# Dealing the token columns of a hybrid decoder step anew: where meta tokens and samples sit

## The reference, cut to what matters

```
h   = rmsnorm(x)                                    # all tokens
p   = h @ w_in                                      # q_a f_a i_a g_a | conv q,k,v | a b | z | gate_a gate_b
o_a = gated linear recurrence (HGRN2) of q_a, f_a, i_a      # prompt in chunks, samples one step
o_b = gated delta rule of conv(q,k,v), a, b                 # prompt in chunks, samples one step
mix = (sigmoid(gate_a) * (norm(o_a) silu(g_a)) @ w_oa + sigmoid(gate_b) * (norm(o_b) silu(z)) @ w_ob) @ w_out
x   = x + mix
x   = x + moe(rmsnorm(x))                           # top 4 of 32 experts, SwiGLU
y   = rmsnorm(x)                                    # y_prompt = tokens 16.. of the prompt, y_sample
```

## Time and profile before

| | us |
|---|---|
| three timed executions | 1292.35, 1294.76, 1291.99; median 1292.35 |
| profiled execution, from the first to the last instruction (span) | 1290.7 |
| TensorE busy | 1229.7 (95%) |
| VectorE busy | 511.5 (40%) |
| ScalarE busy | 241.9 (19%) |
| GpSimd busy | 69.2 (5%) |
| bytes moved | 450.59 MB, 349 GB/s over the span |

### The profile page before, as it was taken

The page is one execution under the profiler, slowest core; times in us unless marked ns, Lnnn a source line. Parts: engine busy times, 40 slices in busy tenths (PEclk is TensorE's granted clock), DMA queues, the critical chain, the costliest instruction groups (busy, mean ns, idle before and its releaser), DMA issues.

```text
span 1290.7 us, 19040 instructions
## 1 busy us (share of the span) xinstructions
PE 1229.7 (95%) x7387; PEld 554.9 (43%) x7387; DVE 511.5 (40%) x1055; ACT 241.9 (19%) x411; POOL 69.2 (5%) x149
## 2 busy tenths in 40 slices
PE   7999989989999999999999999999999999999996
PEld 5887756655433333333333333333333333333331
DVE  1183776254554333333333333333333333333345
ACT  3223611321611111111111111111111111111103
POOL 3002002001210000000000000000000000000001
PEclk9999999999999999999999999999999999999999
DMA  9343307419799999999999999999999999999991
GB/s 305 132 141 129 133 7 208 173 52 365 303 397 408 429 429 427 429 430 429 427 429 430 429 427 429 430 429 427 429 429 429 427 429 429 429 427 430 428 429 70
DMA packets 60854, 450.59 MB, mean 349 GB/s; under 512 B 9234, under 2 KB 18568, under 8 KB 35880
## 3 DMA queue, kind: packets, MB, share of 16 engines
q1 hardware_dynamic: 55748, 446.17, 83.7%
q10 hardware_dynamic: 5068, 3.89, 1.2%
HBM read 443.88 MB, written 6.26 MB: 349 GB/s over the span
## 4 chain that ended last, share of the span: by engine, by line
DMA 41%; PE 25%; DVE 2%; issue 2%; SPq 0%; ACT 0%; DVEq 0%; ACTq 0%
DMA ring<-in_w_gu 41%; PE ps L1070 17%; PE ps L1100 4%; PE ps L1033 1%; PE ps L1010 1%; DVE x_tok L1859 1%; PE ps L1049 1%; DVE proj L1834 0%; DVE proj L1828 0%; PE ps L1057 0%; DVE x_tok L1925 0%; PE ps L1024 0%; SPq L390 0%; DVE feat L1833 0%; PE ps L1041 0%
## 5 line engine op out<-in xcount | busy, mean ns | idle before, releaser
L1070 PE MATMUL ps<-ring,feat 128*64 128x512 f32 x1568 | 355.5, 595 | 22.2 <-DMA ring<-in_w_gu 21.9
L1100 PE MATMUL ps<-ring,proj 128*64 128x512 f32 x992 | 237.7, 601 | 0.0
L1070 PEld LDWEIGHTS ps<-ring,feat 128*64 128x64 f32 x1568 | 107.9, 136 | 205.8 <-issue 169.5
L1859 DVE TENSOR_TENSOR x_tok<-x_tok,ps 96x512 f32<-96x512 f32 x192 | 122.7, 679 | 79.9 <-PE ps L1033 77.1
L1827 DVE TENSOR_SCALAR proj<-ps 128x512 f32<-128x512 f32 x32 | 22.1, 691 | 304.8 <-PE ps L1070 303.8
L1100 PEld LDWEIGHTS ps<-ring,proj 128*64 128x64 f32 x992 | 62.1, 136 | 109.6 <-issue 101.8
L1368 ACT ACTIVATE proj<-ps,wide 128x512 f32<-128x512 f32 x32 | 22.0, 687 | 433.1 <-DVE wide L1842 423.1
L661 PE MATMUL ps<-feat,ring 128*128 128x280 f32 x384 | 97.0, 404 | 0.0
L629 PE MATMUL ps<-feat,ring 128*128 128x280 f32 x384 | 93.5, 406 | 0.2 <-DVEq L1434 0.2
L629 PEld LDWEIGHTS ps<-feat,ring 128*128 128x128 f32 x384 | 74.1, 194 | 19.1 <-DVE feat L1433 0.5
L661 PEld LDWEIGHTS ps<-feat,ring 128*128 128x128 f32 x384 | 71.2, 191 | 19.6 <-issue 3.3
(11 more groups left out here) (383 smaller groups left out, 1084.2 us busy)
## 6 DMA issues: line engine op xcount, KB each, us to landing
ring<-in_w_gu SPq DMA_DIRECT2D x96, 2048.0 KB, 25.0
ring<-in_w_down SPq DMA_DIRECT2D x62, 2048.0 KB, 23.4
proj<-in_w_gu SPq DMA_DIRECT2D x15, 2048.0 KB, 25.9
states<-in_w_gu SPq DMA_DIRECT2D x15, 2048.0 KB, 24.9
ring<-in_w_in SPq DMA_DIRECT2D x11, 2048.0 KB, 8.8
ring<-in_w_gu SPq DMA_DIRECT2D x4, 1024.0 KB, 7.7
ring<-in_w_in SPq DMA_DIRECT2D x2, 1024.0 KB, 8.6
out<-states SPq DMA_DIRECT2D x1, 2048.0 KB, 8.7
```

Source lines behind the costliest of these rows:

```text
L1070: last = mm(bank(j // 2)[64 * (j % 2):64 * (j % 2) + 64, :], xgT[:, k % 4, k // 4, :], w[:, 512 * j:512 * j + 512], start=False, stop=k == ...
L1100: last = mm(bank(y)[64 * j:64 * j + 64, :], h[:, k % 4, 64 * (k // 4):64 * (k // 4) + 64], w[:, n:n + 512], start=False, stop=k == KT - 1)
L1859: tt(x, x, bank(banks[i][j])[0:TP, :], ALU.add).then_inc(sg["comb_taken"], 1)
```

## The change

Columns are dealt anew: 8 empty ones, the 16 meta tokens (from `S0` = 8), the 8 samples (from `SA` = 24), the 256 of the prompt (from `SE` = 32). Still 288 columns and nine chunks. What only makes queries or gates (the chunks in `QUERY`, the output tiles, the merge) works on the 264 columns from `SA`. Mix, router, experts and stores see three tiles of 128, 128 and 8 rows (`ROWS`), taken in the order samples, tile 0, tile 1 (`TILES`). The samples' decays are zeroed in the chunk that they share with the meta tokens, the convolution's history is copied over them, and chunk 0 gives no outputs but the samples'. Blocks beyond one per expert are at most 16 in place of 18. Besides, Sync loads expert 0's third pair and down ahead of the wait for the output tiles, the order of the mix is rewritten, the bias transfers are issued ahead of step B's copies on ScalarE, the store of the sample states ahead of chunk 8, `less(0)` stands between merges, GpSimd's constants are made as soon as step B is done, and the router's selection of tile pairs is done tile by tile.

```diff
-    LEAD = 16
-    S0 = LEAD - NS
-    T = LEAD + NM + SEQ
+    S0 = 8
+    SA = S0 + NM
+    SE = SA + NS
+    T = SE + SEQ
...
+    TQ = T - SA
...
+    X_ROWS = (128, 128, SE)
+    X_COL = (SE, SE + 128, 0)
+    QUERY = (0, 3, 7, 8, 9, 10, 11)
+    ROWS = (128, 128, NS)
+    TILES = (2, 0, 1)
+    TOK = (0, 128, 256)
...
+        def first_col(n):
+            return SA if ORDER[n // 4] in QUERY else S0
...
-            sp.wait_ge(sg["oab_done"], KT)
...
-            for q in range(2):
-                gu_load2(0, q)
-
             sp.wait_ge(sg["gB_done"], NCH)
-            sp.wait_ge(sg["prompt_stored"], 32)
             gu_load2(0, 3)
             sp.wait_ge(sg["conv_stored"], 144)
             for q in range(2):
                 down_load(0, q)
-            sp.wait_ge(sg["merged_ready"], KT)
+            sp.wait_ge(sg["oab_done"], KT)
+            for q in range(2):
+                gu_load2(0, q)
+            sp.wait_ge(sg["wout_lo_used"], 1)
+            gu_load2(0, 2)
+            sp.wait_ge(sg["mix_done"], 5)
+            spare_load(1, 0)
+            sp.wait_ge(sg["lg_done"], NI)
             spare_load(1, 1)
-            sp.wait_ge(sg["mix_done"], 2 * NI)
-            gu_load2(0, 2)
...
-                sp.dma_start(y_prompt[0, 2 * TP - 32:2 * TP + 64, 512 * j:512 * j + 512], x_tok[:, NI - 1, 512 * j:512 * j + 512]) \
-                    .then_inc(sg["out_stored"], 16)
-            sp.wait_ge(sg["out_stored"], 16 * (NI + 2))
+            sp.wait_ge(sg["f_ready"], 2)
+            sp.dma_start(y_prompt[0, 0:128, :], x_tok[:, 0, :]).then_inc(sg["out_stored"], 16)
+            sp.wait_ge(sg["f_ready"], 3)
+            sp.dma_start(y_prompt[0, 128:256, 0:512], x_tok[:, 1, 0:512]).then_inc(sg["out_stored"], 16)
+            sp.wait_ge(sg["f_rest"], 1)
+            sp.dma_start(y_prompt[0, 128:256, 512:D], x_tok[:, 1, 512:D]).then_inc(sg["out_stored"], 16)
+            sp.wait_ge(sg["f_ready"], 4)
+            sp.wait_ge(sg["f_rest"], 2)
+            sp.dma_start(y_sample[:, 0, :], x_tok[0:NS, 2, :]).then_inc(sg["out_stored"], 16)
+            sp.wait_ge(sg["out_stored"], 64)
...
+            for g0, g1, n in ((Q_, F_, SA), (F_, G_, S0), (G_, QB_, SA), (QB_, Z_, S0), (Z_, NFT, SA)):
+                L(gp.memset(proj[:, g0:g1, 0:n], 0.0))
...
-            pool.wait_ge(sg["prompt_stored"], 32)
-            pool.wait_ge(sg["oab_done"], KT)
-            pool.wait_ge(sg["merged_ready"], KT)
+            pool.wait_ge(sg["vnew_done"], NCH)
+            pool.wait_ge(sg["oB_done"], NCH)
+            pool.wait_ge(sg["gB_done"], NCH)
             iot = lambda out, pattern, base, mult: L(gp.iota(out, pattern=pattern, base=base, channel_multiplier=mult,
                                                              allow_small_or_imprecise_dtypes=True))
+            L(gp.memset(lower, -1.0))
+            for q in range(2):
+                masked(lower[:, q:q + 1], [[0, 1]], -NE * (q + 1), 1)
+            gp.sem_inc(sg["route_consts"], 1)
...
+                    last = mm(bank(4 + n % 4)[:, 0:T - c0], win_buf[n // 4 % NRING][:, k, 128 * (n % 4):128 * (n % 4) + 128],
+                              feat[:, k, c0:T], start=k == 0, stop=k == KT - 1)
                 last.then_inc(sg["ptile_done"], 1)
...
-            for n in range(NCH):
+            for n in range(1, NCH):
...
-                    last = mm(bank(b)[:, 0:TN], w[:, k, 128 * m:128 * m + 128], proj[:, g + k, S0:T], start=k == 0, stop=k == H - 1)
+                    last = mm(bank(b)[:, 0:TQ], w[:, k, 128 * m:128 * m + 128], proj[:, g + k, SA:T], start=k == 0, stop=k == H - 1)
...
-                    attend(0, v_new0)
-                    sample_read(4, False).then_inc(sg["oB_done"], 1)
+                    sample_read(4).then_inc(sg["oB_done"], 1)
...
-            def mix(b, t0, t1, j, k0, k1):
+            def w_mix(k, d0, n):
+                return (wout_lo[:, k, :] if k < 4 else wout_hi[:, k - 4, :])[:, d0:d0 + n]
...
+            def mix(i, j, k0, k1):
                 for k in range(k0, k1):
-                    last = mm(bank(b)[0:t1 - t0, :], feat[:, k, t0:t1], w_mix(k, j), start=k == 0, stop=k == KT - 1)
+                    last = mm(bank(4 * i + j), feat[:, k, SE + 128 * i:SE + 128 * i + 128], w_mix(k, 512 * j, 512),
+                              start=k == 0, stop=k == KT - 1)
...
+            def mix_samples(k0, k1):
+                for k in range(k0, k1):
+                    for g in range(4):
+                        last = mm(bank(3)[C * g:C * g + NS, 0:256], feat[:, k, SA:SE], w_mix(k, 256 * g, 256),
+                                  start=k == 0, stop=k == KT - 1)
...
             for j in range(2):
-                mix(j, 0, 128, j, 0, 4)
-            pe.wait_ge(sg["wout2_in"], 16)
+                mix(0, j, 0, 4)
             pe.wait_ge(sg["merged_ready"], KT)
             for j in range(2):
-                mix(j, 0, 128, j, 4, KT)
-            mix_pair(2, 128)
+                mix(1, j, 0, 4)
+            mix_samples(0, 4).then_inc(sg["wout_lo_used"], 1)
+            pe.wait_ge(sg["wout2_in"], 16)
+            mix_samples(4, KT).then_inc(sg["mix_done"], 1)
+            mix(0, 0, 4, KT)
+            turn_samples()
+            mix(0, 1, 4, KT)
+            logits(0)
+            mix(1, 0, 4, KT)
             for j in range(2):
                 turn_x2(0, j)
-            mix(4, 2 * TP, T, 0, 0, KT)
-            for j in range(2):
-                turn_x2(1, j)
-            logits(0)
-            mix(5, 2 * TP, T, 1, 0, 4)
+            mix(1, 1, 4, 6)
+            turn_x2(1, 0)
             logits(1)
-            turn_x2(2, 0)
...
+            mix(1, 1, 6, KT)
+            pe.wait_ge(sg["route_consts"], 2)
+            count_ranks(0)
+            count_ranks(1)
+            turn_x2(1, 1)
...
             L.tell(f(wideh(1), ps[:, 0:H, 0:T], ACT.Copy, scale=-1.0), "wT_taken")
+            for p in range(3):
+                act.dma_start(b_f32[NE * p:NE * p + NE, 0:2 * D], b_gu[0]).then_inc(sg["bias_in"], 16)
+                act.dma_start(b_f32[NE * p:NE * p + NE, 2 * D:3 * D], b_down[0]).then_inc(sg["bias_in"], 16)
...
-            act.dma_start(gdn_sample[0].rearrange("b h k v -> k (b h) v"), states[:]).then_inc(sg["stB_stored"], 16)
+                    act.dma_start(gdn_sample[0].rearrange("b h k v -> k (b h) v"), states[:]).then_inc(sg["stB_stored"], 16)
...
-            for p in range(3):
-                act.dma_start(b_f32[NE * p:NE * p + NE, 0:2 * D], b_gu[0]).then_inc(sg["bias_in"], 16)
-                act.dma_start(b_f32[NE * p:NE * p + NE, 2 * D:3 * D], b_down[0]).then_inc(sg["bias_in"], 16)
...
-            act.wait_ge(sg["prompt_stored"], 32)
...
             def less(i):
                 dve.wait_ge(sg["b3_ready"], i + 1)
                 L.tell(stt(out=b_f32, in0=b3, scalar=lower[:, i:i + 1], in1=b_f32, op0=ALU.mult, op1=ALU.add),
                        "b3_less", i + 1)
 
+            for m in range(KT):
+                t0 = proj[:, VB_ + m % 2, SA:T]
+                dve.wait_ge(sg["oab_done"], m + 1)
+                L(tt(t0, bank(m)[:, 0:TQ], proj[:, GB_ + m, SA:T], ALU.mult))
+                L.tell(tt(feat[:, m, SA:T], t0, proj[:, GA_ + m, SA:T], ALU.add), "merged_ready", m + 1)
+                if m == 4:
+                    dve.wait_ge(sg["route_consts"], 1)
+                    less(0)
+            less(1)
...
+            dve.wait_ge(sg["route_consts"], 2)
+            add_samples()
+            root(0)
             add_mix(0, 0)
+            dve.wait_ge(sg["route_in"], 32)
             add_mix(0, 1)
-            less(1)
+            select(0)
+            root(1)
...
             add_mix(1, 0)
+            take_xT(1)
+            select(1)
             add_mix(1, 1)
...
-            take_xT(0)
-            dve.wait_ge(sg["route_in"], 32)
-            root(0)
-            root(1)
-            add_mix(2, 0)
-            take_xT(1)
-            select(0)
-            select(1)
-            L(ts(selb[:, 0:2], selm[:, 0:2], FAR, -FAR, ALU.mult, ALU.add))
```

546 lines of the change are left out of this document (281 added, 265 removed).

## The result

| | before | after |
|---|---|---|
| median of the timed executions, us | 1292.49 (4 runs) | 1300.99 (4 runs: 1299.54 to 1302.28) |
| span of the profiled execution | 1290.7 | 1298.1 |
| start of the output tiles / of the mix | 289.06 / 304.23 | 286.12 / 300.44 |
| gate_up(0) starts | 353.42 | 353.75 |
| first slot given back | 355.40 | 357.43 |

The changed kernel is slower: ratio 1.0057, 95% interval 1.0045 to 1.007. I had forecast 1283.2 with a range up to 1289.2; the measured time lies outside it and on the other side, where I had put 0.05.

The account below looks back on a forecast made before the run. The expert-weight stream, started by gate_up(0), was taken to fix the end; 4.35 us up to the output tiles, 4.0 in the mix and 0.8 at the end sum to 9.15, giving 1283.2 us, range 1279.5 to 1289.2.

Parts of the forecast that it names:

- (e): Step B: six bias transfers moved on ScalarE's queue delay v_new; 3.1 us lost, bounds 2.6 and 5.3.
- (f): Mix: fewer matmul passes and a new order bring gate_up(0) 4.0 us earlier, bounds 0.5 and 4.4.
- (g): Expert loop: same bytes and passes, 128 rows cost VectorE no more than 96; zero change.
- slower rival: Expert loop: TensorE becomes the bound, in combine and add_back of `down`; needs 1.2 us more an expert; chance 0.05.
- the marks at the end: Mix: mix(1,1) ends at 339.5, last logits at 342.9, select(2) at 344.65, gate_up(0) 4.8 us behind select's last TENSOR_REDUCE.
- (a) to (d): Ahead of the mix, gains: narrower columns 5.1 us, output tiles 1.5, first chunk 0.45, start 0.4.
- my terms for that part: Column gains: 2.6 us up to 164.5 us, 0.4 in step A before 178, 1.3 to 226.5.
- The stream follows gate_up(0): Weight stream: the last prefill lands about 4.4 us sooner and the first slot returns 4.0 sooner, so gate_up(0) sets it.
- (h): Program end: one 32 KB store behind the last norm in place of two; 0.8 us gained, bounds 0.3 and 1.2.

Follow-up runs that it names:

- pad128: Changed kernel with the samples' tile given 128 contraction rows, zeros behind the eighth, in the expert loop's pick_rows and turn_share; 1292.4 us, 0.9987 to 1.0008 of before.
- fill_wait: Changed kernel plus four unused matmuls of 128 rows by 512 columns in TensorE's wait in the mix; 1299.15 us.
- warm: all3 plus unused dense matmuls: five of 256 columns in chunk 7 of step B, three of 512 near the last transposes and logits(2); 1286.46 us.
- best3: best1 plus two unused matmuls of 512 columns, behind the ranks of tile 0 and in the middle of logits(2); 1282.53 us.
- all3: Changed kernel with the loop's samples' tile padded to 128 rows, bias transfers issued by Sync, and take_xT(2) copied before the places; 1284.51 us.
- xt_first: Changed kernel with VectorE's copy take_xT(2) put ahead of place(0) and place(1); 1298.41 us, 1.0027 to 1.0049 of before.
- bias_early: Kernel before with the six bias transfers issued on ScalarE right behind wT_taken; 1298.65 us, 1.0031 to 1.0062 of before.
- best2: best1 with the changed kernel's VectorE order and the 12 row-picking matmuls for the first expert between the halves of logits(2); 1285.46 us.
- nocols: all3 without the narrower projection tiles, all 48 at 280 columns again; 1288.51 us, 0.9954 to 0.9986 of before.
- best1: all3 with the samples' tile also at 128 contraction rows in the rows picked ahead of the loop; 1279.18 us, again 1280.44.

## Why the prediction was wrong, point by point

By spans: forecast 9.15 us gained, measured 7.4 lost, a miss of 16.6. About half of it came ahead of the loop (gate_up(0) at 353.75, forecast 345.1: steps (e) and (f)) and half in the loop (8.0 by pad128: step (g)).

- **(g) Expert loop, the largest step that failed.** "Same bytes, same passes of 512 columns; 128 rows in place of 96 cost VectorE nothing ... Zero." I counted passes and looked at VectorE, and not at what a third tile of 8 rows, put between two of 128, does to TensorE's matmuls: 0.96 us an expert. pad128 gives 8.0 us of span for it. I had found TensorE to be 23.5 us ahead of the stream at 1199.36; 26 steps of 0.96 (25.0) and an end of the first of them 5.5 later (447.36, before 441.90) are 30.5, so that mark comes 7.0 later, at 1206.35. My slower rival had the right bound (TensorE) and the wrong place (`down`) and price (1.2 us an expert as threshold). That threshold took the full 8.35 us of earlier start for granted; without it 0.96 was enough. (Its 1301 for 1.5 us more is also too low by its own terms: 29 x 1.5 less 23 and 8.35 is 12.2 us, 1304.5.)
- **(f) The mix.** Forecast 4.0 sooner, measured 4.1 longer (53.3 against 49.2). The terms that I had worked out stood: first halves 13.8, samples 3.6 (314.26 to 317.90; forecast 3.5). The Trainium skill's 2.38 for three column tiles (page "TensorE: Matmul & The Clock Gate", section "Measured speedup vs the span model") would have made it 4.4, an estimate; the row decides for full overlap of four. What failed are the marks at the end, and that I took the clock's 1.00 for granted. Counted from the first mix matmul, the last mix piece ended at 36.0 us (forecast 35.3), the last logits at 42.1 (38.7), and gate_up(0) started at 53.3 (45.2). In fill_wait, warm and best3 dense matmuls in that stretch kept the clock at 1.00 for longer. That thin work alone brings it down is not shown, since the kernel before held it through the end of its mix. Why VectorE's copy came late: `place(0)`'s first operation took 1.70 us while GpSimd worked, and ended with GpSimd's operation (339.01 and 338.97); in all3 and xt_first it took 0.18. That the two hinder each other there was seen, not tested.
- **(e) Bias transfers.** The step was right in kind and sized too low: forecast 3.1 lost, 2.77 of issues measured, but 6.35 in all (bias_early) and 5.8 in the changed kernel (from 219.72, 6.8 sooner than before, to 300.44, 3.8 sooner, with 2.75 of gains on the way). Where the issues are gone and the clock holds (all3, best2), the way from the end of the start to the output tiles is 249.1 us in place of 254.7, 5.6 less. The missing half is the clock behind the wait.
- **(a) to (d) Columns, output tiles, start.** From the end of the start (31.43; before 33.90) to 219.72 (before 226.52) TensorE gained 4.3 us; my terms for that part were 2.6 + 0.4 + 1.3 = 4.3. nocols gives 4.9 for the whole, forecast 5.1. The start gained 2.5 and not 0.4, but 2.1 of it is the first group of 48 records (11.56 against 13.70), in which TensorE's clock rose late before and ahead of it after (last section). That went either way in runs of one kernel, so I call it luck, though the code before took 13.70 to 13.76 in all three of its traces. The end of the output tiles was forecast 299.9 and measured 300.44: near, because this and the mis-sized (e) cancelled.
- **The stream follows gate_up(0)**: held. bias_early moved gate_up(0) by 6.35 and the span by 6.2.
- **(h) End**: 0.8 forecast, 1.25 measured (from the last group of `combine_last` to the end 12.29 against 13.54).

With both faults mended and VectorE's copy moved (best1) the time is 1279 to 1280, which is better than I had forecast for the change. Without (e) the sum of the other terms is 12.25 us, and best1 gains 12.4 and 13.9; that they are near is in part luck, as its mix is still 2.9 us over the forecast.

## What to carry to other kernels

When a tile is cut so that a small rest is left, ask for each matmul that loops over the tiles how many rows it contracts, and how many its neighbours in TensorE's order do. Here every change between 128 rows and 64 or fewer cost about 0.1 us, and a rest of 8 rows filled up with zeros to 128 cost less than 8 rows. Price a wait of TensorE not only by its length: what follows may run at half clock, and here it did so behind a stretch of many narrow matmuls without a wait as well (xt_first). And spare time in a loop is a budget that every later edit draws on: compute it without the gains that the same change is to bring.

## What the runs showed of the hardware that I had not expected

- Pairs of matmuls side by side in 64 output rows (512 columns, bf16) took 0.22 us a pair with 96 or 128 contraction rows. A pair with 8, 32 or 64 rows among those of 128 made the sequence 0.24 or 0.25 us longer, though its two matmuls started 3 ns apart: the weights for it, and for the pair behind it, were not loaded while the pair ahead ran.
- The granted clock fell where TensorE was 98% busy with narrow matmuls (xt_first), and for equal work it fell in one kernel and held in another that stood a few us elsewhere (277 to 281 before and 284 to 287 in bias_early). Equal kernels differ by it: of the 78 executions of the kernel before that were timed beside the experiments, the 27 with a mean granted clock of 0.997 or 0.998 took 1291.9 us on average, 13 with 0.992 took 1295.2, five with 0.990 or 0.991 took 1298.2.
- The first 48 records of the projection took either 11.56 us or 13.1 to 13.8 (11.56 and 13.11 in the two traces of one kernel, best1). What decides it is when TensorE's clock rises at the start. Its first record at 1.00 begins at 12.2 to 13.4 us in the traces with 11.56, ahead of the group, and at 17.1 to 18.4 in the others, inside it; until about then the records of the group follow each other by 0.47 us, afterwards by 0.24. The windows print 1.00 where there is no record of the clock yet, so only the counts of PE tell it, here 5 against 10 (first the kernel before, then the changed one):

```profile
14.00:16.00 2.00, 2.00 (x5) 1.47 (x6) 0.34 (x3) 1.98 (x5) 1.85 (x2) 1.00 1.04 354
...
14.00:16.00 2.00, 2.00 (x10) 1.60 (x9) 0.08 (x1) 1.97 (x5) 1.49 (x2) 1.00 1.04 339
```
